# Chunked attention: values and turning back for two score rounds at once, with loads of queries and keys released by the scores

## The reference, cut to what matters

```python
# group B: 8 heads, chunks of 64, own + 8 previous chunks, relative bias
sc = einsum('bnchd,bnlhd->bnhcl', qc, kb) * HEAD_DIM ** -0.5 + bias
p = softmax(where(valid, sc, NEG_INF))
ob = einsum('bnhcl,bnlhd->bnchd', p, vb)
# group A: 8 query heads on 2 key/value heads, own + 1 previous chunk, one sink per head
m = maximum(max(sc), sink)
p = exp(sc - m); p = p / (sum(p) + exp(sink - m))
oa = einsum('bnvgcl,bnlvd->bncvgd', p, vb)
```

## Time and profile before

| | |
|---|---|
| median of 3 runs | 2818.0 us (2814.7 to 2821.2) |
| profiled execution, its own time | 2820.7 us |
| its span | 2818.9 us |
| PE busy, share of the span | 2724.2 us, 97% |
| DVE, ACT, POOL busy | 1554.0, 1043.8, 1077.3 us |
| attention stage, about | 532 to 912 us of the span |
| first score of B, first score of A, last score | 532.6, 746.2, 902.6 us |
| mean granted clock of PE over the span | 0.986 |

### The profile page before, as it was taken

The page is one execution under the profiler, slowest core; times in us unless marked ns, Lnnn a source line. Parts: engine busy times, 40 slices in busy tenths (PEclk is TensorE's granted clock), DMA queues, the critical chain, the costliest instruction groups (busy, mean ns, idle before and its releaser), DMA issues.

```text
span 2818.9 us, 40503 instructions
## 1 busy us (share of the span) xinstructions
PE 2724.2 (97%) x14774; PEld 2266.3 (80%) x14774; DVE 1554.0 (55%) x2361; ACT 1043.8 (37%) x2069; POOL 1077.3 (38%) x818
## 2 busy tenths in 40 slices
PE   9999999999877999999998999999999999999998
PEld 9888888788766788888886888888888887888876
DVE  3355664677754332333336766668766666654354
ACT  6433333466654221333324333334333333222242
POOL 7645444210000111321215654555654553552152
PEclk9999999999988999999999999999999999999999
DMA  8657767544444434122226332335432335644454
GB/s 280 240 184 253 264 211 263 169 142 146 131 134 137 179 134 170 61 89 76 68 76 224 103 101 92 113 112 187 127 98 92 107 112 188 239 142 141 140 176 136
DMA packets 260105, 425.38 MB, mean 151 GB/s; under 512 B 18256, under 2 KB 157520, under 8 KB 258896
## 3 DMA queue, kind: packets, MB, share of 16 engines
q1 hardware_dynamic: 222512, 355.29, 38.3%
q10 hardware_dynamic: 37408, 67.65, 7.6%
HBM read 282.35 MB, written 135.27 MB: 148 GB/s over the span
## 4 chain that ended last, share of the span: by engine, by line
PE 55%; DVE 2%; DMA 1%; POOL 1%; ACT 1%; issue 1%; SPq 0%; POOLq 0%; ACTq 0%; DVEq 0%
PE gu_acc L51 9%; PE gu_acc L52 9%; PE gu_acc L53 9%; PE down_acc L51 4%; PE down_acc L53 4%; PE down_acc L52 4%; PE cross_sum_o L51 2%; PE cross_sum_s L51 2%; PE cross_sum_s L53 2%; PE cross_sum_o L53 2%; PE cross_sum_o L52 2%; PE cross_sum_s L52 2%; DVE gu_t L2534 0%; PE cross_turned L2212 0%; PE cross_turned L1930 0%
## 5 line engine op out<-in xcount | busy, mean ns | idle before, releaser
L51 PE MATMUL gu_acc<-gu_t,shared_m 128*128 128x512 f32 x704 | 274.7, 390 | 5.7 <-DVE gu_t L2534 5.7
L53 PE MATMUL gu_acc<-gu_t,shared_m 128*128 128x512 f32 x704 | 274.0, 389 | 0.0
L52 PE MATMUL gu_acc<-gu_t,shared_m 128*128 128x512 f32 x704 | 273.9, 389 | 0.0
L350 POOL TENSOR_TENSOR front_wq_lo<-front_wq_raw,front_wq_hi 128x1024 fp32r<-128x1024 f32 x72 | 179.3, 2491 | 200.3 <-ACT front_wq_hi L346 200.1
L2477 ACT ACTIVATE shared_m<-kept_x 128x512 fp32r<-128x512 f32 x175 | 109.4, 628 | 211.3 <-PE gu_acc L53 190.6
L51 PEld LDWEIGHTS gu_acc<-gu_t,shared_m 128*128 128x128 f32 x704 | 132.1, 188 | 36.3 <-issue 5.4
L53 PEld LDWEIGHTS gu_acc<-gu_t,shared_m 128*128 128x128 f32 x704 | 132.1, 188 | 27.6
L52 PEld LDWEIGHTS gu_acc<-gu_t,shared_m 128*128 128x128 f32 x704 | 132.1, 188 | 27.1
L1494 PE MATMUL att_sum_s<-head_h 64*128 64x320 f32 (+5 forms) x1056 | 105.1, 333 | 42.7 <-DMA att_v<-v_d 24.7
L346 ACT ACTIVATE front_wq_hi<-front_wq_raw 128x1024 fp32r<-128x1024 f32 x72 | 76.2, 1058 | 184.6 <-PE qkv_acc L53 98.9
L51 PE MATMUL gu_acc<-shared_m 128*128 128x512 f32 x352 | 138.0, 392 | 2.9 <-POOL shared_m L2450 2.5
(11 more groups left out here) (353 smaller groups left out, 7627.7 us busy)
## 6 DMA issues: line engine op xcount, KB each, us to landing
front_wq_raw<-in_w_in ACTq DMA_DIRECT2D x69, 512.0 KB, 4.1
head_h<-qk_d SPq DMA_DIRECT2D x48, 512.0 KB, 4.5
ahead_w_even<-in_w_gate SPq DMA_DIRECT2D x44, 512.0 KB, 4.4
kept_x<-in_w_up SPq DMA_DIRECT2D x44, 512.0 KB, 4.3
a_d<-gu_a_mix SPq DMA_DIRECT2D x88, 256.0 KB, 3.2
a_d<-gu_a SPq DMA_DIRECT2D x66, 256.0 KB, 4.2
kept_x<-in_w_down SPq DMA_DIRECT2D x56, 256.0 KB, 4.8
shared_m<-a_d SPq DMA_DIRECT2D x19, 704.0 KB, 4.3
```

The source lines that it names most:

```text
L51: pe.matmul(out, l_hi, r_hi, start=first, stop=False)
L52: pe.matmul(out, l_hi, r_lo, start=False, stop=False)
L53: return pe.matmul(out, l_lo, r_hi, start=False, stop=last)
L350: pool.tensor_tensor(self.lo[:, i % Q_SLOTS, :], self.raw[:, i % Q_SLOTS, :], raw(self.hi[:, i % Q_SLOTS, :]), ALU.subtract).then_inc(self ...
```

## The change

`values`, `copy_o`, `turn_out` and `divide` take a batch of two steps, b = steps 2b and 2b+1. PE runs values of a batch in every even step, behind the score, and turn_out in every odd step, between turn and score. ACT and DVE do copy_o and divide in odd steps. turned_sb gets four buffers instead of two, the small arrays for maxima and sums eight places (SLOTS) instead of four, and o_sb and the bank region of the turned output are twice as wide. score, maxima, exp, turn and copy stay one step at a time, at their places.

On SP, load is split: load(Q) brings queries and keys and waits until the scores of quarter Q-3 are through (s_s); load_v(Q) follows in the queue, with a semaphore of its own (s_lv), and waits for values: as before for quarters whose ring place was last used in a B job, and otherwise for the first half of quarter Q-3. PE waits for values in `values` and no longer in `score`.

The diff, without the renaming of ring places from 4 to SLOTS and the semaphore counts that follow from it:

```diff
-    loaded = [16 * LOADS * sum(j >= 2 for j in range(Q % 4, Q + 1, 4)) for Q in range(N_QUARTER)]
+    N_VALUES = [2 if JOBS[Q // N_BLK][0] == "b" else 1 for Q in range(N_QUARTER)]
+
+    def landed(Q, values):
+
+        return 16 * sum(N_VALUES[j] if values else LOADS - N_VALUES[j] for j in range(Q % 4, Q + 1, 4) if j >= 2)
+
...
-        turned_sb = room.sb("turned_sb", [P, 2, 2, SW])
+        turned_sb = room.sb("turned_sb", [P, 4, 2, SW])
...
-        o_sb = room.sb("o_sb", [P, 2, 2 * P])
+        o_sb = room.sb("o_sb", [P, 2, 4 * P])
...
-        o_turned = turned[2][:, 2 * P:4 * P]
+
+        def o_turned(b):
+            return turned[2][:, (0 if is_a(2 * b) else 2 * P):4 * P]
+
+        def tokens_of(b):
+            return STEPS[2 * b][1] + STEPS[2 * b + 1][1]
...
         def copy(engine, instruction, s, j, part):
 
-            after(engine, s_o, 2 * units(s - 1) if s >= 1 else 0)
+            after(engine, s_o, 2 * units(s - 3) if s >= 3 else 0)
             engine.wait_ge(s_t[j], fillings(s, j) + 1)
             if j == 2:
-                after(engine, s_ot, s - 1)
+                after(engine, s_ot, (s - 1) // 2)
...
-            instruction(turned_sb[:, s % 2, heads[0]:heads[-1] + 1, at:at + w],
+            instruction(turned_sb[:, s % 4, heads[0]:heads[-1] + 1, at:at + w],
...
                 def load(Q):
...
-                    cols, at, s_in = slice(z * BANK, (z + 1) * BANK), slice(z * BT, (z + 1) * BT), s_ld[Q % 4]
+                    cols, s_in = slice(z * BANK, (z + 1) * BANK), s_ld[Q % 4]
...
-                    v_to = v_t[Q % V_RING]
...
-                        for h in range(2):
-                            sp.dma_start(v_to[:, h, :, :], v_d[2 + 2 * x + h, :, at, :]).then_inc(s_in, 16)
...
-                        sp.dma_start(v_to[:, 0, :, :], v_d[head, :, at, :]).then_inc(s_in, 16)
+
+                def load_v(Q):
+                    J, z = divmod(Q, N_BLK)
+                    kind, x = JOBS[J]
+                    at, v_to = slice(z * BT, (z + 1) * BT), v_t[Q % V_RING]
+                    for h in range(N_VALUES[Q]):
+                        sp.dma_start(v_to[:, h, :, :], v_d[2 + 2 * x + h if kind == "b" else x // 2, :, at, :]
+                                     ).then_inc(s_lv[Q % 4], 16)
...
                 for Q in range(3, N_QUARTER):
-                    sp.wait_ge(s_o, 2 * BT * (Q - 2))
+                    sp.wait_ge(s_s, 2 * BT * (Q - 2))
                     load(Q)
+                    sp.wait_ge(s_o, 2 * BT * (Q - 2) if Q - 4 < N_PAIR * N_BLK else 2 * (BT * (Q - 3) + 2))
+                    load_v(Q)
...
-                    after(act, s_out, s - 3)
+                    after(act, s_out, (s - SLOTS) // 2 + 1)
...
-                def copy_o(s):
-                    after(act, s_ot, s - 1)
-                    act.wait_ge(s_o, 2 * units(s + 1))
-                    n = len(STEPS[s][1]) * P
-                    act.activation(o_sb[:, s % 2, 0:n], sum_o[:, 0:n], ACT.Copy).then_inc(s_o_sb, 1)
+                def copy_o(b):
+                    after(act, s_ot, b - 1)
+                    act.wait_ge(s_o, 2 * units(2 * b + 2))
+                    n = len(tokens_of(b)) * P
+                    act.activation(o_sb[:, b % 2, 0:n], sum_o[:, 0:n], ACT.Copy).then_inc(s_o_sb, 1)
...
                 for step in range(NS + 4):
-                    if step >= 4:
-                        copy_o(step - 4)
+                    if step >= 5 and step % 2 == 1:
+                        copy_o((step - 5) // 2)
...
-                def divide(s):
-
-                    J, tokens = STEPS[s]
-                    n = 2 * len(tokens)
-                    denominator = total[:, s % 4, 0:n]
...
+                def divide(b):
+
+                    J, tokens, s = STEPS[2 * b][0], tokens_of(b), 2 * b
+                    n, pair = len(tokens), slice(s % SLOTS, s % SLOTS + 2)
+                    denominator = total[:, pair, 0:n]
                     if is_a(s):
-                        dve.wait_ge(s_whole, s - A0 + 1)
-                        denominator = whole[:, s % 4, :]
+                        dve.wait_ge(s_whole, s + 2 - A0)
+                        denominator = whole[:, pair, :]
                     else:
-                        dve.wait_ge(s_exp, 2 * units(s + 1))
-                    dve.reciprocal(share[:, s % 4, 0:n], denominator).then_inc(s_den, 1)
-                    dve.wait_ge(s_ot, s + 1)
+                        dve.wait_ge(s_exp, 2 * units(s + 2))
+                    dve.reciprocal(share[:, pair, 0:n], denominator).then_inc(s_den, 1)
+                    dve.wait_ge(s_ot, b + 1)
                     if tokens[0] == 0 and J >= 2:
                         dve.wait_ge(s_st[J % 2], 16 * (J // 2))
-                    dve.wait_ge(s_den, s + 1)
-                    dve.tensor_tensor(out[:, J % 2, tokens[0]:tokens[-1] + 1, :].rearrange("p i (h c) -> p (i h) c", c=HD),
-                                      o_turned[:, 0:n * HD].rearrange("p (h c) -> p h c", c=HD),
-                                      share[:, s % 4, 0:n].unsqueeze(2).to_broadcast([P, n, HD]),
+                    dve.wait_ge(s_den, b + 1)
+                    dve.tensor_tensor(out[:, J % 2, tokens[0]:tokens[-1] + 1, :]
+                                      .rearrange("p (j i) (h c) -> p j (i h) c", j=2, c=HD),
+                                      o_turned(b)[:, 0:n * P].rearrange("p (j h c) -> p j h c", j=2, c=HD),
+                                      share[:, pair, 0:n].unsqueeze(3).to_broadcast([P, 2, n, HD]),
                                       ALU.mult).then_inc(s_out, 1)
...
-                    if step >= 4:
-                        divide(step - 4)
+                    if step >= 5 and step % 2 == 1:
+                        divide((step - 5) // 2)
...
-                            pe.wait_ge(s_ld[Q % 4], loaded[Q])
+                            pe.wait_ge(s_ld[Q % 4], landed(Q, False))
                     after(pe, s_max, 2 * units(s))
...
                         pe.wait_ge(s_exp, 2 * (units(s) + j) + x + 1)
                         after(pe, s_copied[b], fillings(s, b))
                         if b == 2:
-                            after(pe, s_out, s - 2)
+                            after(pe, s_out, (s - 2) // 2)
...
-                def values(s):
-
-                    J, tokens = STEPS[s]
-                    for b in range(3):
-                        after(pe, s_copied[b], fillings(s + 1, b))
-                    after(pe, s_o_sb, s)
...
-                def turn_out(s):
-                    pe.wait_ge(s_o_sb, s + 1)
-                    after(pe, s_out, s)
-                    after(pe, s_copied[2], fillings(s + 2, 2))
...
+                def values(b):
+
+                    for bank in range(3):
+                        after(pe, s_copied[bank], fillings(2 * b + 2, bank))
+                    after(pe, s_o_sb, b)
+                    for s in (2 * b, 2 * b + 1):
+                        J, tokens = STEPS[s]
+                        if tokens[0] % BT == 0 and quarter(s) >= 2:
+                            pe.wait_ge(s_lv[quarter(s) % 4], landed(quarter(s), True))
...
+                            w, to = tiles(s, j), (s % 2 * len(tokens) + j) * P
+                            for y in range(w):
+                                tile = i + 1 - w + y
+                                v_at = v_t[(J * N_BLK + tile // BT) % V_RING]
+                                at = j * A_FULL + y * P
+                                for x in range(2):
+                                    last = pe.matmul(sum_o[x * HD:(x + 1) * HD, to:to + P],
+                                                     v_at[:, 0 if is_a(s) else x, tile % BT, :],
+                                                     turned_sb[:, s % 4, x, at:at + P],
+                                                     start=y == 0, stop=y == w - 1)
+                                    if y == w - 1:
+                                        last.then_inc(s_o, 1)
...
+                def turn_out(b):
+                    pe.wait_ge(s_o_sb, b + 1)
+                    after(pe, s_out, b)
+                    after(pe, s_copied[2], fillings(2 * b + 3, 2))
+                    for n in range(len(tokens_of(b))):
+                        last = pe.transpose(o_turned(b)[:, n * P:(n + 1) * P], o_sb[:, b % 2, n * P:(n + 1) * P],
                                             ident[:, :])
...
                 for step in range(NS + 4):
                     if 2 <= step < NS + 2:
                         turn(step - 2)
-                    if step >= 4:
-                        turn_out(step - 4)
+                    if step >= 5 and step % 2 == 1:
+                        turn_out((step - 5) // 2)
                     if step < NS:
                         score(step)
-                    if 3 <= step < NS + 3:
-                        values(step - 3)
+                    if step >= 4 and step % 2 == 0:
+                        values((step - 4) // 2)
```

(36 more changed lines are left out.)

13 lines of the change are left out of this document (6 added, 7 removed).

## The result

| | before | after |
|---|---|---|
| median of the runs | 2819.6 us (2814.7 to 2825.4) | 2788.6 us (2787.4 to 2790.6) |
| profiled execution, its own time | 2820.7 us | 2788.5 us |
| span | 2818.9 us | 2786.8 us |
| first score to first A score (B) | 213.7 us | 227.6 us |
| first A score to last score (A) | 156.3 us | 109.9 us |

The ratio is 0.989, with a 95% interval from 0.987 to 0.991: 31 us less, where 27 were forecast (2791, in the range of 2778 to 2814). It is 1.1% faster, clear of the noise, and for the reason given, with a loss beside the gain. In the experiments one of the four executions of the kernel with the loads alone took 8291.5 us, three times the others; its ratio leaves that one out, and without it the median is 2761.2 us instead of 2761.7.

The account below looks back on a forecast made before the run. PE was taken as the bound, losing time in A to DMA waits and a low clock. 2820.7 - 56.5 + 11.3 + 18.5 = 2794.0 us profiled, less 2.7 for the median: 2791, range 2778 to 2814.

Parts of the forecast that it names:

- step 1: Loads of queries and keys in A: earlier release removes all 14 DMA waits and the low clock, winning 56.5 us.
- step 2: On PE, values and turning back taken two steps at once: saves 0.29 us a pair of steps.
- step 3: PE's new order: scores wait for maxima, opening a gap per pair, costing 18.5 us in B and 11.3 in A.
- the wait for the maxima: Sign in PE's waits: scores waiting on DVE att_top replace the DMA rows, some 48 times, 40 to 50 us.
- rival d: PE's gaps are twice as long through delayed ACT exponentials, some 0.6 us more per pair; 2820 us; chance 0.09.
- (a): Clock in both halves doesn't hold with regular idle gaps on PE, falling to 0.83; 2833 us, slower; chance 0.10.
- (b): Loads in A still come late, half of the 56.5 us stays; 2809 us; chance 0.06.
- (c): Gaps on PE before the scores don't arise, because DVE gets ahead; 2748 us; chance 0.03.

## Why the prediction was right, point by point

**The loads (step 1).** Right. No DMA wait is left, and the clock in A is 1.00. The lead was enough: in the changed kernel SP issues queries and keys of one quarter from 786.76 us on, and the score that needs them starts at 798.81, 12.0 us later, where the schedule had 12.1 less 1, that is 11.1. The term was too small. The prediction had 56.5 us to win, and the loads alone won 61.0 in A. Three of these 4.5 us are a miscount: the stretch of 152.9 us begins at the second score of A (749.68), the first being at 746.2, and so holds 30 steps and not 31; with 93.3 instead of 96.4 us at full speed the term would have been 59.6. The rest is that the first steps of each job are narrower than the 3.11 us taken for all: 95.3 us for 31 steps are 3.07.

**The saving on PE (step 2).** Right in kind, a little too large. In the rows above forty values take 2.33 us (674.60 to 676.93), where twice twenty take 2.48: 0.15, not 0.19. Turning out saves 0.11 in B and 0.09 in A. That is 0.25 us a pair instead of 0.29. But it isn't a gain at all, since the order that gives it opens a larger gap; and the part that could be had without a gap, the turns out, is paid again as 0.1 us more between turn and score (the kernel with values one step at a time).

**The gap (step 3).** Right, in place, in cause and nearly in size. In B a job has 6.5 us of gaps (1.02, 0.96, 0.71, then 0.80 and 0.71 in turn) where the prediction had 6.9, and is 4.1 us longer instead of 4.6. B as a whole is 13.9 us longer than before instead of 18.5. The job that begins the stage is the difference: it is only 1.3 us longer than in the execution shown before, and 2.8 longer than with the loads alone. Its first steps waited for the maxima before, too. The 1.5 us between the two numbers are hardly an effect of the change: in the execution shown before, the clock came up later at the start of B (0.63 from 538.3 to 546.0 us, against 0.89 over the same steps with the loads alone). With values one step at a time it came up as late (0.63), so executions seem to differ in this. Against the loads alone B is 15.4 us longer, and that is the better measure of this term. In the last B job one bracket says 1.15 us where the other jobs have 0.80; there the maxima waited 0.67 us for an exponential on ACT (716.77). In A the second score starts 4.32 us after the first turn, not 4.24:

```profile
780.06 1.10 PE L1533 MATMUL att_turned<-wout_ident,att_probs_a 128*128 128x128 f32 x8
780.99 0.60 PE L1565 MATMUL att_turned<-wout_ident,att_o_sb 128*128 128x128 f32 x4
781.52 0.92 PE L1514 MATMUL att_sum_s<-head_h 64*128 64x192 f32 x12
782.37 1.43 PE L1533 MATMUL att_turned<-wout_ident,att_probs_a 128*128 128x128 f32 x8
784.38 0.92 PE L1514 MATMUL att_sum_s<-head_h 64*128 64x192 f32 x12 [0.59 <-DVE att_top L1457]
785.23 1.97 PE L1553 MATMUL att_sum_o<-att_turned_sb,head_h 128*64 128x128 f32 x32
787.13 1.10 PE L1533 MATMUL att_turned<-wout_ident,att_probs_a 128*128 128x128 f32 x8
```

The division of 512 columns took 0.69 us and 0.60 to the next start, as the widths had it (0.61). The reciprocal and the wait for it took 0.07 more, and four maxima are 0.34 apart instead of 0.33. The pair takes 7.07 us instead of 6.95, 14.6 us over 15.5 pairs against the loads alone, instead of 11.3. One of the signs named beforehand missed: the wait for the maxima was to be 40 to 50 us in all, and the profile has 30.5. Its brackets leave out some 0.17 us of each gap, by the overlap of matmuls, and in A another 0.3, for which the turn before it was itself held up (rival d). Together these are some 12 us, so that the gaps themselves were about as long as forecast.

**The sum.** -56.5, +11.3 and +18.5 make -26.7; a profiled execution had -32.2. By the same stretches it is -61.0 and +14.6 in A, -1.5 and +15.4 in B: -32.5. The first score came 2.7 us later in the execution shown after, and what follows attention made up for it. The errors of the terms in A cancel to 1.2 us; the larger part of the miss is B. That the median was met within 2.4 us, where the profiled execution was missed by 5.5, is luck in part: the prediction took off 2.7 us for what the execution shown before lies above its median, but with a fourth run this is only 1.1, and the execution shown after lies on its median.

**The rivals.** (a) The clock held: 1.00 in A and 0.98 in B, as before. Its idle stretches, most of 0.5 to 0.7 us and none over 1.15, at a beat of 7 to 8 us, didn't change it. So what the Trainium skill says of frequent short idle times ("TensorE: Matmul & The Clock Gate", section "A second HAM failure mode: psum-queue depth-cycling") does not come true at this length; with the extra operation, at 1.1 us and more, it begins to (last section). Of the 36.5 us by which B and A grew there, five falls of the clock at 1.6 us each are 8. That leaves 28.5 for 46 operations, four of them long; 46 x 0.60 and 3.4 for the long ones would be 31. A few of them are not paid in full: a pair of narrow steps early in a job grew by 0.2 us. (b) Didn't happen. (c) Didn't happen; what takes the gap away is work on PE, by the kernel with values one step at a time. (d) It is there, but inside the gap: of the rows of A above the second turn takes 1.43 us instead of 1.10, 0.3 us more. That it waits for exponentials on ACT is said by the profile only where a row is split, as here:

```profile
797.50 0.66 PE L1533 MATMUL att_turned<-wout_ident,att_probs_a 128*128 128x128 f32 x4 [0.23 <-ACT att_probs_a L1381]
```

It costs nothing as long as DVE is later, except at the one place in the last B job, 0.35 us. With the division moved away it is next.

## What to carry to other kernels

Before work of one engine is put together to save the start of its series, look what it stood between: here values covered the time from a score to its maxima, and the batch saved 0.25 us a pair and opened a gap of 0.7 to 1.1. Where a kernel changes two things, cost them apart and then together: the loads alone are 27 us better than both, and the batch alone is 40 us worse than neither, because it moves the event on which the loads were released. Release a buffer by its own last reader, queries and keys by the scores and not by the values, and see what stands before the load in its queue.

## What was not expected of the hardware

A DVE operation that reads two inputs from SBUF (512 columns, float32) takes 0.68 us by itself. Where it met a POOL subtraction it took 1.33 to 2.05 us, eight times in the two kernels that have it, and each time it ended 0.54 to 0.56 us after the subtraction did: 677.43 against 676.88 in the rows above. The subtraction, which had begun first each time, kept its 2.4 us. So DVE stood still until POOL was through. The maxima and the copies of DVE, which read PSUM, keep their 0.82 and 0.69 us beside the same subtractions. The Trainium skill ("SBUF — State Buffer", section "Terms") says that VectorE and GpSimd share a pair of ports, held by one of them for a whole instruction; the rows agree.

The clock stood nearly all of the regular gaps, and no length can be given at which it falls. In the kernel with the extra operation, B has gaps of 1.1 to 1.2 us at a beat of 8.4 us, and the clock is 1.00 behind each of them. Three gaps of 1.7 us brought it down once, those of 1.9 to 2.0 us two times in three, and one of 1.6 us didn't. But in A it fell behind a gap of 1.51 us, and behind one of 1.15 us, of the same kind as its neighbours:

```profile
792.94 1.37 PE L1520 MATMUL att_sum_s<-head_h 64*128 64x192 f32 x12 [1.51 <-DVE att_top L1458]
878.09 1.20 PE L1520 MATMUL att_sum_s<-head_h 64*128 64x128 f32 x12 [1.15 <-DVE att_top L1458]
```

Twelve score matmuls take 0.92 us elsewhere. With the gaps of the changed kernel it didn't happen, although one of them is 1.15 us as well (718.23, in B).
